# Attention values in two passes per head, the second head counted backward, and latent values for two pairs at once

## The reference, cut to what matters

```python
# branch A, per head: strictly causal, no softmax
z = q @ k.T * SB_SCALE
log_1mb = where(visible, log_sigmoid(-z), 0)
suffix = cumsum(log_1mb, reverse=True) - log_1mb
a = where(visible, exp(log_sigmoid(z) + suffix), 0)
o_A = a @ v                                     # 8 heads x 64
# branch B, per head: latent attention, block-causal
s = (q_lat @ c_kv.T + q_rope @ k_rope.T) * MLA_SCALE
o_B = (softmax(where(visible, s, -inf)) @ c_kv) @ w_uv
mix = (sigmoid(gate_a) * (o_A @ w_proj_sb) + sigmoid(gate_b) * (o_B @ w_proj_mla)) @ w_out
```

## Time and profile before

| | |
|---|---|
| median of 3 runs | 1851.74 us |
| profiled execution | 1851.8 us, span of its instructions 1850.0 us |
| PE busy | 1829.1 us (99%), 14262 matmuls and transposes |
| DVE, ACT, POOL busy | 927.8, 559.8, 1074.3 us |
| chain that ended last | PE 92%, DVE 5%, ACT 1% |
| granted TensorE clock | 1.0 in all slices |
| L1563, the projections | 76% of the chain |
| value products L1726 and L1722 | 52.4 and 16.5 us busy |

### The profile page before, as it was taken

One profiled execution on the slowest core, in us unless ns is written; L12 is line 12 of the kernel. 1 busy time (PEld: TensorE's weight loads), 2 busy tenths in 40 slices (PEclk: granted clock), 3 DMA queues, 4 the chain that ended last, 5 costly groups with the idle time before them and its releaser, 6 DMA issues.

```text
span 1850.0 us, 33796 instructions
## 1 busy us (share of the span) xinstructions
PE 1829.1 (99%) x14262; PEld 1773.7 (96%) x14262; DVE 927.8 (50%) x1634; ACT 559.8 (30%) x1197; POOL 1074.3 (58%) x996
## 2 busy tenths in 40 slices
PE   9999999999999999999999999999999999999999
PEld 8999989999999999999999999899999999999999
DVE  6676775232755532523556767752346555235143
ACT  4444443112422211202344444430133222112021
POOL 8685534746555555556666854446456555555564
PEclk9999999999999999999999999999999999999999
DMA  5242112233223222223343421212422222222222
GB/s 188 88 136 73 63 41 81 92 118 115 70 91 92 83 89 92 86 80 97 98 143 93 127 86 47 69 62 88 152 80 75 86 92 89 84 92 92 80 83 95
DMA packets 76231, 170.49 MB, mean 92 GB/s; under 512 B 6384, under 2 KB 34160, under 8 KB 76080
## 3 DMA queue, kind: packets, MB, share of 16 engines
q1 hardware_dynamic: 68752, 160.79, 27.2%
q10 hardware_dynamic: 7328, 7.54, 1.2%
HBM read 156.41 MB, written 9.79 MB: 90 GB/s over the span
## 4 chain that ended last, share of the span: by engine, by line
PE 92%; DVE 5%; ACT 1%; issue 0%; POOL 0%; DMA 0%; SPq 0%; DVEq 0%; ACTq 0%; POOLq 0%
PE ps L1563 76%; PE ps L1598 2%; PE ps L1726 2%; PE ps L1684 2%; DVE xT L1430 1%; DVE xn L1091 1%; DVE mix L1427 1%; PE ps L1775 1%; PE ps L1781 1%; PE ps L1637 1%; PE ps L1703 1%; DVE R L1091 1%; DVE xT L1248 1%; PE ps L1652 1%; PE ps L1749 1%; PE ps L1722 1%
## 5 line engine op out<-in xcount | busy, mean ns | idle before, releaser
L1563 PE MATMUL ps<-xn,wsp 128*128 128x272 f32 x7824 | 1002.4, 289 | 4.2 <-issue 2.2
L1563 PEld LDWEIGHTS ps<-xn,wsp 128*128 128x128 f32 x7824 | 985.4, 189 | 8.2 <-issue 4.1
L612 POOL CAST wsp<-raw 128x1024 fp32r<-128x1024 f32 (+2 forms) x222 | 219.0, 991 | 505.9 <-DMA raw<-in_wstream 452.1
L619 POOL TENSOR_TENSOR wsp<-raw,wsp 128x1024 fp32r<-128x1024 f32 (+2 forms) x278 | 492.3, 1782 | 16.2
L1563 PE MATMUL ps<-R,wsp 128*128 128x272 f32 x3840 | 486.2, 288 | 0.1
L1563 PEld LDWEIGHTS ps<-R,wsp 128*128 128x128 f32 x3840 | 482.7, 189 | 1.2 <-DVE xT L1120 0.5
L606 POOL TENSOR_TENSOR wsp<-raw,wsp 128x256 fp32r<-128x256 f32 x304 | 240.3, 811 | 12.2
L601 POOL CAST wsp<-raw 128x512 fp32r<-128x512 f32 x152 | 106.3, 699 | 151.8 <-DMA raw<-in_wstream 116.1
L1091 DVE SCALAR_TENSOR_TENSOR R<-ps,R 64x256 fp32r<-64x256 f32 (+11 forms) x264 | 129.8, 510 | 72.2 <-ACT R L749 24.9
L1446 DVE TENSOR_TENSOR mix<-ps,rstd 128x272 f32<-128x272 f32 x88 | 38.8, 441 | 202.5 <-PE ps L1563 192.2
L976 ACT ACTIVATE mix<-vv 128x2 f32<-128x2 f32 x88 | 18.0, 204 | 363.0 <-DVE mix L1448 363.0
(11 more groups left out here) (230 smaller groups left out, 1543.0 us busy)
## 6 DMA issues: line engine op xcount, KB each, us to landing
raw<-in_wstream SPq DMA_DIRECT2D x233, 512.0 KB, 3.5
raw<-in_wstream SPq DMA_DIRECT2D x48, 128.0 KB, 2.7
raw<-in_wstream SPq DMA_DIRECT2D x16, 384.0 KB, 3.1
raw<-in_kc SPq DMA_DIRECT2D x8, 512.0 KB, 3.8
raw<-in_vc SPq DMA_DIRECT2D x8, 512.0 KB, 4.4
xT<-in_x_in SPq DMA_DIRECT2D x8, 272.0 KB, 5.0
out_k_out<-mix ACTq DMA_DIRECT2D x8, 272.0 KB, 2.9
xT<-in_x_in SPq DMA_DIRECT2D x1, 2176.0 KB, 9.3
```

Of the source, the lines that this page charges most:

```text
L612: ins = nc.gpsimd.tensor_copy(dst[:, 0, f], part[:, f])
L619: ins = nc.gpsimd.tensor_tensor(dst[:, 1, f], part[:, f], dst[:, 0, f].bitcast(F32), ALU.subtract)
L1563: mm = pe.matmul(z[:, h], w[:, x, (k0 + k) * P:(k0 + k + 1) * P], rhs[:, y, k, h * HT:(h + 1) * HT], start=(k == 0 and (x, y) == (0, 0)), ...
```

## The change

Weights and values. The transposed weights `at` get one region per head: per key block, all query blocks that see it lie side by side, for the second head counted backward, so that one matmul per key block takes 512, 384, 256 or 128 columns of one head. The values are stored with high and low part side by side (64 + 64 columns), so that one weight load holds both. `pv` now works on one head: for each key block one matmul with the high weights and one with the low. In the bank, partitions 0 to 63 hold the products with the high values and 64 to 127 those with the low values; ACT copies the upper half out, DVE subtracts that copy and then adds the lower half. The product low x low is now included. `pv0` stands 5 steps behind the pair's first unit, and `pv1`, the second head, right behind it (`second`), or, in steps 9 and 18, between the first and the later filling quarters (`midst`). In steps behind a sample unit of branch B (`sooner`, step 35) DVE and ACT empty both before the maxima.

Latent values. `kv` only makes the keys and takes one bank; `vv` makes the values of two pairs with matmuls of 256 columns, in steps 20 and 29.

Order. Quotas of fillers change in steps 3, 5, 6, 8, 12 to 17, `ot(0)` moves from step 14 to 12, `kv(1)` from 20 to 19. In branch B's steps with value products ACT does the exponents before the high weights.

```diff
@@ tables @@
-        AHEAD = {start(br, t) + d: [("pv" + h + br, t)] for br in "sm" for t in range(PAIRS) for h, d in (("a", 3), ("b", 5))}
+        AHEAD = {start(br, t) + 5: [("pv0" + br, t)] for br in "sm" for t in range(PAIRS)}
+        SECOND = {s: [("pv1" + n[3], t)] for s, ((n, t),) in AHEAD.items()}
-                      [4, 4, 4, 3, 3, 3, 4, 4, 3, 4, 4, 4, 3, 2, 3, 2, 3, 3] +
+                      [4, 4, 4, 4, 3, 1, 4, 4, 4, 4, 4, 4, 4, 2, 2, 2, 3, 3] +
+        def midst(s):
+            return second(s) if s <= NS and sample(s - 1) else []
+        def sooner(s):
+            return s > NS and sample(s - 1)
@@ weights and values @@
-            o = qb * (qb + 1) // 2 * P
-            return at[:, x, :, o:o + P * (qb + 1)]
+            a = at[:, x, qb * P:(qb + 1) * P]
+            return bass.AP(tensor=a.tensor, offset=a.offset,
+                           ap=[a.ap[0], [(2 * ATW // P - 1 - 5 * qb) * P, 2], [3 * P, qb + 1], [1, P]])
+        def at_keys(x, r, kb):
+            o = (2 * ATW // P - 4 - 3 * kb if r else 4 * kb) * P
+            return at[:, x, o:o + (QB - kb) * P]
@@ ACT, high weights of the next pair @@
-                        elif t > 0 and qb in (0, 2):
-                            act.wait_ge(S["p_done"], AT[(("pva" if qb == 0 else "pvb") + br, t - 1)] + 1)
+                        elif t > 0 and qb == 0:
+                            act.wait_ge(S["p_done"], AT[("pv1" + br, t - 1)] + 1)
@@ ACT, order of a step @@
+                        for t in second(s) if sooner(s) else []:
+                            evacuate(t, s)
+                        if NS <= s < NU and second(s):
+                            exponents(s)
                         if s > 0:
                             weights_hi(s - 1)
-                        if NS <= s < NU:
+                        if NS <= s < NU and not second(s):
                             exponents(s)
@@ DVE, emptying a value product @@
-                        for r in range(2):
-                            lo(o[64 * r:64 * r + 64, 1, t[1], q], bank(t)[64 * r:64 * r + 64, 256 * r:256 * r + 256],
-                               o[64 * r:64 * r + 64, 0, t[1], q], "dve_read" if r else None)
+                        lo(turned(o[:, 1], 0), turned(z[0:64], r), turned(o[:, 0], 0), "pv_low")
+                        dve.wait_ge(S["pv_low"], PV_AT[t] + 1)
+                        v.tensor_tensor(turned(o[:, 1], 0), turned(z[64:128], r), turned(o[:, 1], 0).bitcast(F32),
+                                        ALU.add).then_inc(S["dve_read"], 1)
@@ PE, the value product @@
-                        for kb in range(blocks):
-                            for i, (x, y) in enumerate(PARTS):
...
+                        if r == 0:
+                            pe.wait_ge(S["dve_read"], dread(("vt", p) if br == "s" else ("vv", p // 2)))
+                            pe.wait_ge(S["at_lo"], start(br, p) + QB)
+                        for kb in range(QB):
+                            w = (QB - kb) * P
+                            z = bank(t)[:, 0:w] if r else bank(t)[:, 512 - w:512]
+                            for x in range(2):
+                                mm = pe.matmul(z, val[:, 2 * kb + r].rearrange("p x f -> p (x f)"), at_keys(x, r, kb),
+                                               start=(kb == 0 and x == 0), stop=(kb == QB - 1 and x == 1))
@@ PE, latent values @@
+                    def vv_tile(t):
+                        banks_free(t)
+                        p = slice(512 + 2 * t[1] * P, 512 + 2 * (t[1] + 1) * P)
                         for kb in range(QB):
                             for i, (x, y) in enumerate(PARTS):
-                                mm = pe.matmul(bank(t, 1)[:, kb * P:(kb + 1) * P], cT[:, x, kb * P:(kb + 1) * P],
-                                               ukuv[:, y, 512 + t[1] * P:512 + (t[1] + 1) * P], start=(i == 0), stop=(i == 2))
+                                mm = pe.matmul(bank(t, kb // 2)[:, kb % 2 * 2 * P:(kb % 2 + 1) * 2 * P], cT[:, x, kb * P:(kb + 1) * P],
+                                               ukuv[:, y, p], start=(i == 0), stop=(i == 2))
@@ PE, order of a step @@
+                        for t in second(s) if not midst(s) else []:
+                            pv(t)
                         if s > 0:
                             turn(s - 1)
...
-                        quarters(fills(s))
+                        quarters(fills(s)[:1])
+                        for t in midst(s):
+                            pv(t)
+                        quarters(fills(s)[1:])
```

More of the change, by code:

```diff
@@ L312, in ahead, with second @@
             return AHEAD.get(s, [])
+        def second(s):
+            return SECOND.get(s, [])
+        def midst(s):
+            return second(s) if s <= NS and sample(s - 1) else []
+        def sooner(s):
+            return s > NS and sample(s - 1)
         def after(s):
@@ L326, in sample @@
             return 0 <= n < NU and units[n][0] in "SM"
+        PV_AT = {t: n for n, t in enumerate([t for s in range(STEPS) for t in ahead(s) + second(s) if t[0][0:2] == "pv"])}
         EVENTS = []
@@ L347, in build @@
             whole(*ahead(s))
+            whole(*(second(s) if not midst(s) else []))
             if sample(s - 1):
@@ L350, in build @@
             whole(*after(s))
-            some(fills(s))
+            some(fills(s)[:1])
+            whole(*midst(s))
+            some(fills(s)[1:])
         whole(("ya", 0), ("ol", 0))
@@ L764, in kv_tile @@
                         act.wait_ge(S["p_done"], AT[t] + 1)
-                        ac(kn[:, t[1] % 2, 0], bank(t), ACT.Copy)
-                        ac(vm[:, t[1] % 2, 0], bank(t, 1).rearrange("p (b l) -> p b l", l=P),
-                           ACT.Copy).then_inc(S["act_read"], 1)
+                        ac(kn[:, t[1] % 2, 0], bank(t), ACT.Copy).then_inc(S["act_read"], 1)
+                    def vv_tile(t):
+                        act.wait_ge(S["p_done"], AT[t] + 1)
+                        for i in range(2):
+                            ins = ac(by_heads(v_parts(vm, i, 0)), vv_view(t, i), ACT.Copy)
+                        ins.then_inc(S["act_read"], 1)
                     def ql_tile(t):
@@ L1347, in _ @@
                             suffixes(s)
-                        elif s < NU:
+                        elif s < NU and not sooner(s):
                             maxima(s)
-                        for t in ahead(s):
+                        for t in ahead(s) + (second(s) if sooner(s) else []):
                             evacuate(t)
+                        if s < NU and sooner(s):
+                            maxima(s)
                         if s > 0:
@@ L1354, in _ @@
                         if s < NS:
-                            for t in after(s):
+                            for t in (second(s) if not midst(s) else []) + after(s):
                                 evacuate(t)
@@ L1359, in _ @@
                             normalise(s)
-                        for t in (after(s) if s >= NS else []) + [t for t, i in fills(s) if i == 3]:
+                        for t in ((second(s) if not sooner(s) else []) + after(s) if s >= NS else midst(s)) + [t for t, i in fills(s) if i == 3]:
                             evacuate(t)
@@ L1683, in turn @@
                             for kb in range(qb + 1):
[L1684 removed]
+                                j = qb - kb if r else kb
+                                mm = pe.transpose(ps[:, ZB + 2 * (n % 2) + r, j * P:(j + 1) * P], x[:, r, kb * P:(kb + 1) * P], ident)
                         mm.then_inc(S["at_tr"], 1)
```

102 lines of the change are left out of this document (57 added, 45 removed).

## The result

The changed kernel takes **1859.96 us** (median of 6 runs, 1855.22 to 1860.14); the kernel before took 1851.74 on the same chip. The ratio is 1.0039, 95% interval 1.0028 to 1.0050: slower by 0.4%, where 1847.2 was forecast and 1854 was the upper end. The profiled execution took 1860.1 with a span of 1858.3 (before: 1850.0), so the span grew by 8.3 us.

The account below looks back on a forecast made before the run. PE's stream plus its waits bounds the kernel (PE 99% busy). 20 us saved, less 15.4 of net new waits (10.6 minus 2.9 relief, 7.7 per layer), leaves 4.6: 1851.8 to 1847.2 us, range 1838 to 1854.

Parts of the forecast that it names:

- What PE saves: Fewer, wider matmuls on PE: value products 16.2 us and latent values 4.6, together 20.8, counted as 20.
- Step 5: PE waits 1.8 us per layer: 1.2 for VectorE's chain, 0.3 for the v turn's scaling, 0.3 for copies delayed by rotation.
- the "0.3" for the rotation moved up to step 3: Part of the wait put at step 5: the rotation now starting in step 3 delays copies by 0.3 us.
- Step 9: Second head's product waits for the first's addition in the same bank, behind rotation and scans: 2.8 us per layer.
- Steps 12, 19, 28, 32, 35: PE waits, us per layer: 12, 1.2; 19's scores, 1.1; 28, 0.7; 32, 0.8; 35, 1.35 and 1.6.
- the rise in step 35: Gate projection and turn wait 2.95 us, of which 1.2 was there before: 1.75 more per layer.
- Step 30: A score waits behind the latent values' copies: 0.3 us per layer.
- the 0.4 of others: Other places with slack near zero: 0.4 us of new waits per layer.
- The relief: Old waits that go, among them scores of steps 28 and 32 and turns of 3 and 12: 2.9 us per layer.
- Rival 2: Two or three more waits (steps 15, 22, 25, 33), or 384 columns cost as 512: 1850 to 1855 us; chance 0.18.
- Rival 3: Slow additions and block-wise copies, 1.02 for 0.68 us, in ten steps awaiting both heads' emptying: +14, 1861 us; chance 0.09.
- Rival 1: Chains have more slack; new waits come to half, 5.3 us per layer: 1837 us, 1826 with none; chance 0.24.

Follow-up runs that it names:

- the kernel of 1836.8: Changed kernel, former quarter numbers except one moved from 19 to 18, step 9's first head emptied before scans, two quarters before its second product, step 35 reordered: 1836.78 us.

## Why the prediction was wrong

**What PE saves: right.** With the clock at 1.00 throughout (the kernel of 1836.8), PE is busy 1829.1 - 1808.9 = 20.2 us less than before, where 20 was counted; the latent values alone gave 4.5 for 4.6; sixteen value matmuls took 2.57 for 2.60.

**Step 5: the first step that failed.** It was put at 1.8 us per layer. It brought 1.63 (scores of step 5) + 1.79 (scores of step 6) + 1.27 (its turn), 4.7 start to start. The turn had been put at 1.2, and that was right. The term that failed is the "0.3" for the rotation moved up to step 3: the sum let VectorE begin step 5 as it did before. But VectorE is nearly full from 75 to 92 us, so the rotation ahead of step 4's scans made everything behind it late, and both steps' scores waited, 3.4 us where 0.3 was counted. The experiments bear this out: with the rotation a step later the scores' waits fall from 6.2 to 1.5 us in both layers and the turn's stays. The fault was to work out each step from its own start; a queue that is full carries its lateness over.

**The clock: the second, a term left at nothing without a reason.** The saving at full clock is 20.2, the busy time of the changed kernel fell by 13.5, so 6.7 us are the half clock's, all in the stretches behind the waits of steps 5, 6 and 9. That is more than step 5's 2 x 2.9. Without it the time would be about 1853.3 (an estimate, 1860.0 - 6.7), just inside the upper end. The Trainium skill ("TensorE: Matmul & The Clock Gate", Part 1) says that an idle array falls back to half its clock and needs busy time to come back; the trace agrees in step 9 (0.50 in 126.0 to 129.5, behind a wait of 3.52); behind the waits of steps 5 and 6 it does so in one layer and not in the other. In the profiled executions PE's busy time, for the same 14182 instructions, tells the clock's part from the waits':

| kernel | PE idle, us | PE busy, us | mean granted clock |
|---|---|---|---|
| changed | 42.7 | 1815.6 | 0.995 |
| rotation a step later | 38.6 | 1814.1 | 0.997 |
| old numbers of quarters | 37.9 | 1810.7 | 0.998 |
| two quarters ahead of the second product | 41.8 | 1812.7 | 0.997 |
| second rotation later | 35.0 | 1813.5 | 0.997 |
| first head emptied ahead of the scans | 36.0 | 1809.2 | 0.999 |
| the kernel of 1836.8 | 26.1 | 1808.9 | 1.000 |

So the old numbers' 9.2 us, 9.7 in the spans, are half waits (4.8) and half clock (4.9).

**Step 9: right mechanism, too small.** 2.8 was taken, 3.7 came. The rotation took 4.15 us (118.88 to 123.03, its last operations 1.14 each), where before showed 3.6 and the forecast took a value between that and an undisturbed rotation of 3.0. Why those operations took 1.14 here and 1.02 before no run shows. Emptying first, or a quarter more ahead of the product, takes the wait down by what it should (3.7 to 2.2 by the quarter, 4.2 to 2.2 by the order, first layer), so PE waits for that bank alone.

**Steps 12, 19, 28, 32, 35: right**, each wait within 0.2 us. Only the rise in step 35 is 2.05 and not 1.75: the forecast took 1.2 off for the wait that stood there, and its own rule (shown idle plus 0.16) gives 0.97. Step 30 and the 0.4 of others didn't come. The relief came as counted: of before's waits 0.32, 0.38, 0.30, 0.47, 0.70 and 0.71 (start to start) are gone in the first layer, 2.9.

Together, per layer: 4.7 + 3.7 + 0.9 + 1.2 + 1.65 + 2.05 - 2.9 = 11.3, two layers 22.6 against 21.8 more idle on the page. The forecast had 15.4, so waits are 6.4 of the miss; with 6.7 for the clock, less 0.2 more saved, that is 12.9 us, the distance of the span (1858.3) from the forecast's (1845.4 = 1850.0 - 4.6).

**The rivals.** Rival 2 named the wrong places (waits it took for zero stayed at zero), but its kind is what happened: more wait, in the two steps already named. Rival 3's mechanism is ruled out: the additions take 0.69 and the head's copies 0.59, and the time came near its 1861 by another way, by luck. Rival 1 fell: the new waits didn't come to half, they came above the count.

What stays open: when the clock falls behind a wait and when not; why it fell behind step 9 in both layers with the rotation a step later and in one with the old numbers; why the rotation's operations took longer; and why the latent values alone wait for a chunk of weights (0.7), for which there is no run.

## What to carry to other kernels

Where a helper engine runs without a gap over several steps, work out its queue over all of them and not each step from its own start; an item that is moved up delays all that stand behind it, for as long as the queue has no gap. Moving filler and an order of emptying is worth as much as the matmuls saved: here 20 us saved were a loss of 8 with one plan of quarters and one order of emptying, and a gain of 15 with another. A wait of some microseconds on TensorE can bring the half clock behind it; here that came or not with equal waits, and cost 6.7 us with four new waits per layer. So an experiment on waits is read by idle and busy time apart, not by the time alone.

## What was not expected of the hardware

Half clock behind waits of quite unlike length, and not behind equal ones. In the changed kernel the three waits of steps 5 and 6 (1.47, 1.63 and 1.16 within 9 us) are the same in both layers, and the clock fell behind them in the first alone. The wait of 2.58 in step 19 (two quarters ahead) had it in the second layer and not in the first; that of 1.83 in step 9, in the second with the second rotation later, in the first with the quarters spread. It came behind single waits of 3.52, 4.02, 2.79 (without the additions, second layer) and 2.07 us (eight matmuls in 2.54), but not behind 3.07 (old numbers, second layer) or 2.03 (1.46). So between 1.8 and 3.1 us the length of the wait doesn't decide it; no run separates what does.
